# Rewriting the mixing stage of a hybrid attention and RWKV-7 block on one core

## What is computed

```python
h = rmsnorm(x, mix_norm)
q, k, v, z_rwkv, gate_a, gate_b = split(h @ w_in)        # 1024 x 6656 weights
zr, zk, zv, uw, ua, ug = split(z + (prev_token(z) - z) * mu)
# A: 16 heads of 64 in 2 kv groups, chunks of 64 queries over 128 keys, ALiBi, a sink per head
# B: RWKV-7, 16 heads, state 64 x 64 per head:
#    sa = state @ a_t
#    state = state * w_t + sa b_t^T + v_t k_t^T ;  y_t = state @ r_t
#    y = group_norm(y) * ln_w + ln_b + (sum r k r_k) v ;  y *= g
merged = sigmoid(gate_a) * A + sigmoid(gate_b) * B
x = x + merged @ w_out
```

## Time and profile before

| | us |
|---|---|
| median of 3 runs | 3914.48 (3913.32 to 3922.29) |
| profiled execution | 3915.28 |
| its span in the trace | 3913.5 |
| TensorE busy | 3518.5 (90%) |
| VectorE busy | 1469.4 (38%) |
| ScalarE busy | 1021.0 (26%) |
| GpSimd busy | 776.1 (20%) |

### The profile page before, as it was taken

The page is one execution under the profiler, slowest core; times in us unless marked ns, Lnnn a source line. Parts: engine busy times, 40 slices in busy tenths (PEclk is TensorE's granted clock), DMA queues, the critical chain, the costliest instruction groups (busy, mean ns, idle before and its releaser), DMA issues. The chain is left out here.

```text
span 3913.5 us, 53024 instructions
## 1 busy us (share of the span) xinstructions
PE 3518.5 (90%) x21022; PEld 2618.0 (67%) x21022; DVE 1469.4 (38%) x2586; ACT 1021.0 (26%) x1775; POOL 776.1 (20%) x462
## 2 busy tenths in 40 slices
PE   4999999988999999898999998768898799999996
PEld 3888888844666666555656665557676678888885
DVE  4222222223545455555555554541322232222224
ACT  2111111111333333333333333322222221111111
POOL 2212121100112111212111111212312232222120
PEclk7999999989999999999999999888899889999998
DMA  3111111021000000000000000006110111111111
GB/s 101 51 46 50 46 50 47 16 70 39 21 21 17 16 20 21 16 21 20 21 15 26 15 21 15 4 16 197 38 32 16 49 49 43 54 43 54 43 38 43
DMA packets 205050, 148.84 MB, mean 38 GB/s; under 512 B 8768, under 2 KB 194240, under 8 KB 204352
## 3 DMA queue, kind: packets, MB, share of 16 engines
q1 hardware_dynamic: 204864, 146.21, 12.0%
HBM read 133.60 MB, written 12.58 MB: 37 GB/s over the span
## 5 line engine op out<-in xcount | busy, mean ns | idle before, releaser
L806 PE MATMUL bank<-work,arena 128*128 128x512 f32 x1536 | 764.7, 613 | 8.7 <-DMA arena<-w_in 8.7
L390 PE MATMUL bank<-h_high,w_high 128*128 128x512 f32 x1408 | 555.0, 394 | 22.7 <-POOL h_low L249 14.5
L390 PE MATMUL bank<-h_low,w_high 128*128 128x512 f32 x1408 | 552.2, 392 | 0.0
L390 PE MATMUL bank<-h_high,w_low 128*128 128x512 f32 x1408 | 552.1, 392 | 0.0
L361 POOL TENSOR_TENSOR w_low<-ffn_work,w_high 128x1024 fp32r<-128x1024 f32 x132 | 319.8, 2444 | 1079.8 <-ACT w_high L419 1079.8
L806 PEld LDWEIGHTS bank<-work,arena 128*128 128x128 f32 x1536 | 261.2, 193 | 170.1 <-issue 160.0
L464 DVE TENSOR_TENSOR ffn_work<-ffn_work,bank 128x512 f32<-128x512 f32 x88 | 60.5, 688 | 813.0 <-ACT ffn_work L427 813.0
L390 PEld LDWEIGHTS bank<-h_high,w_high 128*128 128x128 f32 x1408 | 266.4, 189 | 88.1 <-DVE h_low L249 14.0
L473 DVE SCALAR_TENSOR_TENSOR arena<-bank,arena 128x512 f32<-128x512 f32 x352 | 241.3, 691 | 194.8 <-PE bank L404 194.8
L390 PEld LDWEIGHTS bank<-h_high,w_low 128*128 128x128 f32 x1408 | 267.0, 190 | 55.9
L390 PEld LDWEIGHTS bank<-h_low,w_high 128*128 128x128 f32 x1408 | 267.2, 190 | 54.6
(11 more groups left out here) (246 smaller groups left out, 4978.1 us busy)
## 6 DMA issues: line engine op xcount, KB each, us to landing
arena<-w_in SPq DMA_DIRECT2D x48, 512.0 KB, 3.8
ffn_work<-w_gate SPq DMA_DIRECT2D x44, 512.0 KB, 3.8
ffn_work<-w_up SPq DMA_DIRECT2D x44, 512.0 KB, 3.8
ffn_work<-w_down SPq DMA_DIRECT2D x44, 512.0 KB, 3.3
cross_work<-w_ckv SPq DMA_DIRECT2D x16, 512.0 KB, 4.0
work<-x SPq DMA_DIRECT2D x1, 4096.0 KB, 14.6
x_spill<-arena SPq DMA_DIRECT2D x1, 4096.0 KB, 14.9
m_spill<-work SPq DMA_DIRECT2D x16, 256.0 KB, 2.3
```

The lines of the kernel that those rows point to most:

```text
L390: last = mm(bank[:, 2 * n + b, :], w[wp][:, 2 * f + b, kt], h[hp][:, kt, tok], start=kt + wp + hp == 0, stop=kt == KT - 1 and wp == 1)
L806: last = mm(bank[:, unit % 2, :], panel[j % 3][:, kt], hT[:, kt, n * HALF:(n + 1) * HALF], start=kt == 0, stop=kt == KT - 1)
```

## The change

The mixing stage is written anew; the feed-forward, cross and final stages only take a changed form of the argument that names the two parts of a norm.

- `shared()`: the norm now writes high and low parts (both halves, `hA` and `hB`), the five panels are rounded by ScalarE and subtracted by GpSimd, and each product is three fp32r matmuls. The parts of the second half are written to `h_spill` in HBM (two transfers of 2 MB).
- `mixer()` loops over halves outermost, pairs inside: 16 half-pairs, each with six units of 24 fp32r matmuls over 512 tokens. A panel is loaded again for the second half, so 96 panel loads in place of 48, each followed by a rounding on ScalarE and a subtraction on GpSimd. `h_spill` is loaded back in 16 transfers after the eighth half-pair's units.
- The two heads are stacked rather than put on a diagonal: `heads` issues one 64-row, 64-column matmul for each. The `_bd` copies and the transposes go; token-major copies come from matmuls with a scaled identity.
- The chain of chunks of half-pair `i-1` runs in the same loop body as the preparation of half-pair `i`, with projections of half-pair `i+1` as filling. The body runs 17 times. Nothing is looped by the hardware any more.

```diff
+            FILL = {"start": 6, "p1": 2, "sa": 2, "st": 2, "mid": 6, "s0": 6, "s1": 6, "z": 8, "x": 6, "end": 2}
+            LATE = {"start": 0, "p1": 0, "sa": 0, "st": 0, "mid": 12, "s0": 12, "s1": 12, "z": 12, "x": 9, "end": 3}
+            TERMS = 3 * KT
...
+                    def heads(out, lhs, rhs, start=True, stop=True):
+
+                        for e in range(2):
+                            last = mm(hs(out, e), hs(lhs, e), hs(rhs, e), start=start, stop=stop)
+                        return last
...
-                        last = mm(bank[:, unit % 2, :], panel[j % 3][:, kt], hT[:, kt, n * HALF:(n + 1) * HALF],
-                                  start=kt == 0, stop=kt == KT - 1)
+                        kt, (wp, hp) = m // 3, THREE[m % 3]
...
+                        last = mm(bank[:, unit % 2, :], pw[wp][:, unit % 2, kt], hA[hp][:, kt], start=m == 0,
+                                  stop=m == TERMS - 1)
...
+                        def through_state(n):
+                            seen_back("state_ready", NC, n)
+                            heads(bank[:, C, 0:CH], before[:, n, 0:CH], v_tok[:, n, :], stop=False)
+                            heads(bank[:, C, 0:CH], old[:, n, 0, :], state[:, pb, n % 2, :],
+                                  start=False).then_inc(S("p1_ready"), 1)
...
+                        for n in range(NC):
+                            if back:
+                                through_state(n)
+                                if n > 0:
+                                    outputs(n - 1)
+                            fill("p1")
...
+                            if back:
+                                solve(n)
+                            fill("sa")
+                            if back:
+                                grow_state(n)
+                            fill("st")
...
+                                for m in range(NC):
+                                    last = heads(one(F0)[:, m, :], n_st[:, m, :], xt[:, m, :])
+                                last.then_inc(S("z_ready"), 1)
...
+                            fill("z")
+                            if live:
+                                seen("z_stored", 5, n + 1)
+                                if n == 0:
+                                    seen("x0_ready")
+                                else:
+                                    seen("x_added", 4, n)
+                                for m in range(NC):
+                                    last = heads(one(F1)[:, m, :], x_st[:, m, :], z_st[:, m, :])
+                                last.then_inc(S("xt_grown"), 1)
+                                if n < 4:
...
+                                        last = heads(one(F2)[:, m, :], z_st[:, m, :], x_st[:, m, :])
```

```diff
+                        lows("s1")
+                        if live:
+                            pool.wait_ge(S("n_stored"), i + 1)
+                            joined = by_chunk(diff[0])
...
+                            G.tensor_tensor(x_st[:], joined, over_chunks(c("stack_ident")), ALU.add).then_inc(
+                                S("x0_ready"), 1)
```

More of the change, by code:

```diff
@@ L211, in __init__, with pieces @@
                 Norm.splits += parts is not None
+            def pieces(self, which):
+                n = self.width // len(self.parts[which])
+                return [(t, i * n, n) for i, t in enumerate(self.parts[which])]
             def square(self, act, kt):
@@ L657, in one, with four, __init__ @@
                 return bank[:, bk, :].rearrange("p (c b) -> p c b", b=CH)
[L659 to L683, removed]
+            def four(bk):
+                return bank[:, bk, :].rearrange("p (c b) -> p c b", b=P)
+            F0, F1, F2, F3, C, Y = 2, 3, 4, 5, 6, 7
+            FILL = {"start": 6, "p1": 2, "sa": 2, "st": 2, "mid": 6, "s0": 6, "s1": 6, "z": 8, "x": 6, "end": 2}
+            LATE = {"start": 0, "p1": 0, "sa": 0, "st": 0, "mid": 12, "s0": 12, "s1": 12, "z": 12, "x": 9, "end": 3}
+            TERMS = 3 * KT
             class Filling:
[L688 to L691, removed]
+                def __init__(self, i):
+                    self.at, self.first = 0, NP * (i + 1)
+                    self.fill = {} if i >= ITER - 1 else LATE if i == PAIRS - 1 else FILL
                 def take(self, point):
@@ L788, in _ @@
+                    pool.wait_ge(s_zero, 3)
+                    for unit in range(NP + 2):
+                        subtract_panel(unit)
+                    for i in range(ITER + 1):
+                        body(i)
                 @block.tensor
@@ L966, in body @@
-                            last.then_inc(S("var_scale_ready"), 1)
-                            fill("end")
-                            assert filling.full()
-                    for unit in range(8):
-                        for kt in range(KT):
-                            big(0, unit, kt)
-                    pe.wait_ge(s_zero, 15)
-                    with pe.Fori(0, PAIRS - 1) as p:
-                        body(p, False)
-                    body(PAIRS - 1, True)
+                            fill("p1")
@@ L978, in _ @@
+                        fill("end")
+                        assert filling.full(), filling.at
+                    pe.wait_ge(s_zero, 3)
+                    for unit in range(NP):
+                        for m in range(TERMS):
+                            project(unit, m)
+                    for i in range(ITER + 1):
+                        body(i)
                 @block.scalar
```

1251 lines of the change are left out of this document (689 added, 562 removed).

## The result

The changed kernel takes 3728.05 us (median of 4 runs, 3718.31 to 3730.8), the one before 3916.72 us beside it: a ratio of 0.9513 with a 95% interval of 0.9491 to 0.9534. I had said 3688, in a range of 3540 to 3810.

What follows compares the result with a forecast made beforehand. TensorE's stream and an equally long chain of waits bound the mixing stage. A full body at 80.2 + 4.9 + 1.2 + 2.9 + 3.0 = 92.2 us ended the stage 226 us earlier: 3688 us, range 3540 to 3810.

Steps and rivals of the forecast that it cites:

- The two limits before: Old mixing stage: TensorE's stream fills it and the chain of waits beneath is as long, 104.5 us a half.
- The stream of a full body: TensorE's own matmuls and tile-shape switches in one new mixer body with everything in it: 80.2 us, against 104.5.
- Waits of the chain: VectorE's ordered work lengthens a body's eight chunks from 23.2 to 28.1 us, +4.9 a body.
- pieces A and B: Preparation work on VectorE between the three chain instructions; a chunk then takes about A + B + 1.55 us.
- The squared keys: Top of a body: differences and mix queue behind GpSimd's last panel subtraction, delaying squares and sum; +1.2 us.
- The first level: GpSimd makes `x_st` only after its panel subtraction, later than TensorE's other work there lasts; +2.9 us a body.
- GpSimd stopping VectorE: GpSimd's subtractions hold up VectorE operations in the chain's chunks; +3 us a body, between 0 and 5.
- 0.95 or more until body 15: Sign to look for in the mixer's trace: the clock stays at 0.95 or more until body 15.
- The shared stage: Stage before the mixer's bodies: norm parts pace the first panel, four more at 43.6 us; net -3.5 us.
- TensorE's stream alone: Rival, 17%: interleaving hides the waits, 14 mixer bodies at 81 us, total 3530 to 3570 us.
- The engines holding one another: Rival, 13%: VectorE's waits spread and the clock falls; bodies of 98 to 106 us, total 3830, up to 3890.
- The pair that does not overlap: Rival, 8%: the second head's 64x64 matmul waits for the first, 32 us a body, total about 4150 us.

Runs made afterwards that it cites:

- e10: e5 with one float32 product in place of three fp32r passes in the mixer's projections; 3735.73 us, +123 from e5.
- e9: e5 with the third fp32r pass of every mixer projection left out; 3491.02 us, -122 from e5.
- e5: Changed kernel with both GpSimd moves: first `x_st` ahead of the panel subtraction, next half-pair's differences ahead of the body's last one; 3612.74 us, -115.
- e12: e5 with a chunk's filling passes at two points instead of three and the levels' filling at one point instead of two; 3587.26 us, ratio 0.9161.
- e4: Changed kernel with GpSimd making the next half-pair's differences before the body's last panel subtraction; 3656.32 us, -72.
- e3: Changed kernel with GpSimd making the first `x_st` before the panel subtraction of the same point; 3683.2 us, -45.
- e8: Changed kernel, order kept, with GpSimd subtracting only the first 128 columns of a panel after the first two units, so the output changes; 3613.81 us.
- e2: Changed kernel with one float32 product in place of three fp32r passes in the mixer's projections; 3788.52 us, +60.
- e6: Changed kernel with a chunk's six filling passes at two points (3 and 3) instead of three (2, 2, 2); 3702.12 us, -26.

## Why the prediction was right, point by point

**The two limits before.** That the stage stood at its stream and its chain at once was the reason to count both. No run tests it on the kernel before. e10 and e9 bear it out for the new kernel with the waits gone: three passes as one float32 product cost 7.7 us, and 10.9 us fewer of passes gave 7.9 and new waits for the chain.

**The stream of a full body, 80.2 us.** Taking e5's waits of 1.4 us from its 85.8 leaves 84.4. The rate of the 64x64 pair, the term that decided the sign, was right (0.031 us a record expected, 0.98 us for 32 of them from 1347.54 to 1348.52). The term that was mis-sized is the switch. I took 84 at 0.09 us, 7.6; the trace has 77, and by e12 one costs 0.15, which makes 11.6 and is an estimate. That is 4.0 of the 4.2 us missing. Where a short group stands between two switches, as the four records of `solve`, the cost falls partly behind the group, and I had read it only before one.

**Waits of the chain, +4.9 us.** Measured 1.3 us in a full body, and 1.4 in e5, all for the new state. My pieces A and B of VectorE did not add up: no wait for a copy shows in a full body. The term was 3.6 too large.

**The squared keys, +1.2 us.** Measured 1.7. The cause named, differences and mix behind a panel subtraction, is shown by e4, which moves just that.

**The first level, +2.9 us.** Measured 2.0: the subtraction takes 2.0 us in the mixer and not the 2.44 of the earlier trace rows. The cause is shown by e3.

**GpSimd stopping VectorE, +3.0 us.** I had put it in the chain, under the panel subtractions. This step of the prediction failed. In e5, where they are at full length, all waits of the chain are 1.4 us a body, and in e8 without them 0.8. The stops are real (2.36 us in place of 0.77 for one product), but they fell where TensorE had work. One of another kind, by the differences, lies in the wait at the keys (1.51 in place of 0.74 us); no run takes it away by itself. My row for it was misread, too: the 0.69 us product of the earlier trace rows did not run alone, but started 0.04 us ahead of a mask of GpSimd, while the one of 1.47 started 0.68 us behind one. The product of 2.36 us started 0.18 us behind a subtraction. Who starts first decides here, and I had not asked that.

**What no step had: the clock.** I named the half clock for body 15 and within a rival, not in a full body, and gave 0.95 or more until body 15 as a sign; by its writes a body is at 0.93 to 0.96, and body 7 at 0.81. e4 gained 72 us where all waits at the keys together are about 30. By full bodies in the mean: with the wait at the keys alone left (e3) 91.3 us, with the one at the first level alone (e4) 88.8, with neither (e5) 85.8. So the first costs 5.5 us, 1.7 of waiting and 3.8 of low clock, and the second 3.0, of which 1.0. That is 4.8 us of clock. The full body then reads 84.4 + 1.3 + 1.7 + 2.0 + 4.8 = 94.2 us, against 94.0 measured and 92.2 predicted: the clock's 4.8, 4.2 of stream and 0.5 at the keys too little, 3.0 for GpSimd, 3.6 for the chain and 0.9 at the first level too much, which leaves 2.0. Errors of both signs cancelled: that the sum came so near was luck. That two waits behind GpSimd's subtractions come on top of the stream was not, by e3 and e4.

**The ends.** Body 0 took 79.8 us (78), bodies 15 and 16 together 102.2 (103). Body 7, priced as the others, took 102.9.

**The shared stage.** Predicted 3.5 us less (with a slip: 816.7 and 21 are 837.7, not 838.7); its last product started at 888.88 and the old one ended near 889.8, so it gave under 1 us. The additions of squares took 12.3 us instead of the 8.6 of the earlier trace rows, as foreseen, but the norm's whole sequence then came 5.6 us late, and about the first 14 of its passes ran at half clock. The first projection started at 904.22 where I had 901.6.

**The sum.** 2445.7 against 2403: 4.9 us at the start of body 0, 1.8 in it, 36.4 in the 14 bodies from 1 to 14 (94.6 - 92, body 7 among them), -0.8 at the end. Nothing behind it changed, as said: 1284.4 us from the last write to the end before, 1282.9 after.

**The rivals.** TensorE's stream alone (81 a body) did not come. The engines holding one another came in a mild form, in 4.8 us of clock. The pair that does not overlap is refuted by the trace (`heads` writes both heads into one PSUM bank, and 32 records take 0.98 us): the Trainium skill's rule (TensorEngine Tiling (Array Packing), "Restrictions and Gotchas") is not borne out here for two row halves that write different partitions. The lock that the Trainium skill (SBUF — State Buffer, "SBUF: two separate sides") describes agrees with the product of 2.36 us, which ended 0.55 us behind the end of the subtraction.

What the passes brought is told by e2 and e10: in the changed kernel the mixer's three passes are worth 60 of the 188 us, and with the waits gone 123, where the products alone are priced at 138. Both figures have the 16 switches in them that the float32 product saves. The difference between them is mostly the clock, at 0.99 in e2's full bodies until 1605 us and 0.94 in the changed kernel's.

## What to carry to other kernels

Give a wait of TensorE two prices, its length and the stretch at half clock behind it: here 1.7 us of waiting cost 5.5. Look for it first in the queue of the slowest helper, where an urgent small operation stands behind a bulk one that nobody needs yet; two such reorderings on an engine that was 24% busy gave 115 us. And before reading an ablation as "the other engine binds", look at the clock: taking work away lowered it, and that hid about 4 us a body. Count also what an edit of the filling does to the switches between tile shapes; here e2, e6 and e12 each changed another number of them than I had taken.

## What the runs showed that I had not expected

- Less work on TensorE lowered its clock where waits were already there: 0.94 to 0.88 with a third of the projection passes gone, 0.98 with one float32 product for three passes.
- Two matmuls on the two row halves that write different banks start 0.01 us apart (lines 976 and 977): four records of 512 columns in 1.06 us.
- Four short records between two changes of tile shape take 0.26 us, twice their rate in a long run, and with eight changes fewer a body is 1.2 us shorter.
